# Order of weight and modulation-row requests on SyncE, four row buffers for the gate, and eviction order in group_a

## What is computed

```
shift, scale, gate = split(silu(c) @ w_mod + b_mod)      # w_mod: 2048 x 6144
h  = rms_norm(x) * (1 + scale) + shift
u, g = split(h @ w_in)                                   # 2048 each
pooled_i = window_mean(u_i) - u_i                        # 4 groups of 512 features
y  = (pooled_i @ w_grp_i) * pool_scale
x1 = x + gate * ((y * silu(g)) @ w_out)
x' = rms_norm(x1) * final_g
out = x' + hybrid_layer(x', mem)                         # attention a, b, c; not touched
```

## Time and profile before

| what | value |
|---|---|
| median of 3 runs | 2381.94 us (2381.07 to 2383.51) |
| the profiled execution, its own time | 2384.18 us |
| its span | 2382.6 us |
| mean granted TensorE clock | 0.982 |
| TensorE matmul busy | 2265.2 us, 95% of the span |
| VectorE busy | 1217.7 us, 51% |
| ScalarE busy | 844.8 us, 35% |
| DMA traffic | 280.39 MB, mean 118 GB/s |

### The profile page before, as it was taken

One profiled execution on the slowest core, in us unless ns is written; L12 is line 12 of the kernel. 1 busy time (PEld: TensorE's weight loads), 2 busy tenths in 40 slices (PEclk: granted clock), 3 DMA queues, 4 the chain that ended last, 5 costly groups with the idle time before them and its releaser, 6 DMA issues.

```text
span 2382.6 us, 31373 instructions
## 1 busy us (share of the span) xinstructions
PE 2265.2 (95%) x10156; PEld 1826.7 (77%) x10156; DVE 1217.7 (51%) x2102; ACT 844.8 (35%) x1551; POOL 149.6 (6%) x195
## 2 busy tenths in 40 slices
PE   5798779999899899999999999999999999999999
PEld 4686658887678677777777778888888888887887
DVE  6885567544665744444465656633433333334332
ACT  6433244433234333333344444422222222223221
POOL 0000000001122111111111111000000000000000
PEclk9999889999999999999999999999999999999999
DMA  8664412225643422222222222222222222222443
GB/s 327 242 232 159 174 65 98 98 98 201 236 154 108 148 82 79 76 74 79 71 71 69 73 67 88 84 98 97 97 96 97 96 94 95 96 96 87 148 147 110
DMA packets 74730, 280.39 MB, mean 118 GB/s; under 512 B 8596, under 2 KB 11412, under 8 KB 66208
## 3 DMA queue, kind: packets, MB, share of 16 engines
q1 hardware_dynamic: 68880, 263.59, 32.3%
q0 software_dynamic: 3040, 9.46, 1.1%
q10 hardware_dynamic: 2736, 6.42, 0.7%
HBM read 269.98 MB, written 9.46 MB: 117 GB/s over the span
## 4 chain that ended last, share of the span: by engine, by line
PE 81%; issue 7%; DVE 6%; DVEq 2%; ACT 2%; DMA 1%; ACTq 1%; SPq 0%; POOLq 0%; POOL 0%
PE bank L385 25%; PE bank L387 24%; PE bank L386 24%; DVE w_lo L379 3%; PE bank L467 3%; PE bank L497 2%; PE bank L481 1%; DVEq L374 1%; PE bank L505 1%; ACT w_hi L369 1%; DVE x_lo L1690 1%; DMA w_raw<-stream 0%; DVEq L1605 0%; DMA mem_raw<-mem_features 0%; PE bank L470 0%
## 5 line engine op out<-in xcount | busy, mean ns | idle before, releaser
L385 PE MATMUL bank<-x_hi,w_hi 128*128 128x512 f32 x2896 | 1166.8, 403 | 72.5 <-DVE w_lo L379 41.9
L387 PE MATMUL bank<-x_hi,w_lo 128*128 128x512 f32 x2896 | 1140.7, 394 | 0.0
L386 PE MATMUL bank<-x_lo,w_hi 128*128 128x512 f32 x2896 | 1140.6, 394 | 0.0
L379 DVE TENSOR_TENSOR w_lo<-w_raw,w_hi 128x512 fp32r<-128x512 f32 x692 | 490.2, 708 | 943.4 <-ACT w_hi L369 927.0
L369 ACT ACTIVATE w_hi<-w_raw 128x512 fp32r<-128x512 f32 x692 | 437.2, 632 | 1032.2 <-PE bank L387 920.4
L385 PEld LDWEIGHTS bank<-x_hi,w_hi 128*128 128x128 f32 x2896 | 552.0, 191 | 211.2 <-issue 42.8
L386 PEld LDWEIGHTS bank<-x_lo,w_hi 128*128 128x128 f32 x2896 | 552.4, 191 | 117.4 <-issue 6.3
L387 PEld LDWEIGHTS bank<-x_hi,w_lo 128*128 128x128 f32 x2896 | 551.3, 190 | 118.2
L1334 DVE CUSTOM_DVE_ANT_0 wmod<-wmod,c_rows 128x2048 f32<-128x2048 f32 x48 | 109.7, 2287 | 78.2 <-issue 78.2
L767 POOL TENSOR_TENSOR probs<-probs,rden 128x128 f32<-128x128 f32 (+2 forms) x112 | 79.7, 740 | 550.4 <-DVE rden L654 550.4
L565 ACT ACTIVATE probs<-probs,neg_max 128x128 f32<-128x128 f32 (+2 forms) x112 | 57.9, 517 | 95.5 <-DVE neg_max L642 95.2
(11 more groups left out here) (153 smaller groups left out, 1194.0 us busy)
## 6 DMA issues: line engine op xcount, KB each, us to landing
w_raw<-stream SPq DMA_DIRECT2D x346, 512.0 KB, 3.5
wmod<-w_mod_rows SPq DMA_DIRECT2D x48, 1024.0 KB, 6.6
front_raw<-stream SPq DMA_DIRECT2D x16, 1024.0 KB, 7.4
x<-x_features SPq DMA_DIRECT2D x4, 1024.0 KB, 18.4
x_in<-x_features SPq DMA_DIRECT2D x16, 256.0 KB, 4.7
x_store<-tmp POOLq DMA_DIRECT2D x16, 256.0 KB, 3.0
x_back<-x_store SPq DMA_DIRECT2D x16, 256.0 KB, 4.3
result_features<-result ACTq DMA_DIRECT2D x16, 256.0 KB, 4.1
```

Of the source, the lines that this page charges most:

```text
L379: nc.vector.tensor_tensor(w_lo[:, q, :], raw_quarter(s), w_hi[:, q, :].bitcast(F32), ALU.subtract).then_inc(lo_ready, 1)
L385: nc.tensor.matmul(bank_ap[:, :tokens], hi, x_hi[:, kx, :], start=start, stop=False)
L386: nc.tensor.matmul(bank_ap[:, :tokens], hi, x_lo[:, kx, :], start=False, stop=False)
L387: return nc.tensor.matmul(bank_ap[:, :tokens], lo, x_hi[:, kx, :], start=False, stop=stop)
```

## The change

In pool_u the two row requests of a panel are issued before the panel's load, not behind it. The gate's columns get four buffers (6 to 9) in place of two; at the start of pool_out four row requests are issued at once, and from m = 1 to 6 two each ahead of the panel's load. `c_rows` is kept: sq_b, sum_a and sum_b move into the region that the window sums no longer use, and `c_rows3` goes away with its load and its silu. Column 32 moves from beat (0, 3) to (0, 1). In group_a ScalarE runs `group_out` ahead of the two `h_high`. The variance in forget waits for both sums at once, since it now overwrites the place of sq_b.

```diff
-MOD_SLOT = [m % 4 for m in range(KT + 4)] + [2 + m % 4 for m in range(KT - 4)] + [6 + m % 2 for m in range(KT)]
+MOD_SLOT = [m % 4 for m in range(KT + 4)] + [2 + m % 4 for m in range(KT - 4)] + [6 + m % 4 for m in range(KT)]
...
-        sq_b = sb("sq_b", [P, T], F32, at_upper + 2 * KB)
-        sum_a = sb("sum_a", [P, T], F32, at_upper + 4 * KB)
-        sum_b = sb("sum_b", [P, T], F32, at_upper + 6 * KB)
+        sq_b = sb("sq_b", [P, T], F32, at_scratch + 4 * KB)
+        sum_a = sb("sum_a", [P, T], F32, at_scratch + 6 * KB)
+        sum_b = sb("sum_b", [P, T], F32, at_scratch + 8 * KB)
...
             for i in range(6):
-                load_panel(sp, At(RING + 1 + i))
                 mod_rows(KT + 4 + 2 * i)
                 mod_rows(KT + 5 + 2 * i)
+                load_panel(sp, At(RING + 1 + i))
...
             for m in range(KT):
+                if 0 < m < KT // 2 - 1:
+                    mod_rows(2 * KT + 2 * m + 2)
+                    mod_rows(2 * KT + 2 * m + 3)
                 load_panel(sp, At(FIRST["pool_out"] + 1 + m))
                 if m == 0:
                     sp.wait_ge(w_used, 4 * FIRST["pool_out"])
-                if m < KT // 2:
-                    mod_rows(2 * KT + 2 * m)
-                    mod_rows(2 * KT + 2 * m + 1)
+                    for n in range(4):
+                        mod_rows(2 * KT + n)
...
+                    if 4 * i + s > 0:
+                        group_out(4 * i + s - 1)
                     for k in range(4 + 2 * (4 * i + s), min(KT, 6 + 2 * (4 * i + s))):
                         h_high(k)
-                    if 4 * i + s > 0:
-                        group_out(4 * i + s - 1)
...
                     if m == 0 and s == 0:
                         gate_sigmoid(KT - 1)
-                        act.dma_start(c_rows3[:, :], cvec.to_broadcast([P, D])).then_inc(gate_c_loaded, 16)
                     if m == 0 and s == 1:
                         yg_high(KT - 1)
-                    if m == 0 and s == 2:
-                        act.wait_ge(gate_c_loaded, 16)
-                        nc.scalar.activation(c_rows3[:, :], c_rows3[:, :], ACT.Silu).then_inc(c_ready, 1)
                         act.preload_act_table_set("natural_log_exp_and_others")
...
-                    if m == 0 and s == 3:
-                        dve.wait_ge(c_ready, 2)
-                    if m < KT // 2 and s == (3 if m == 0 else 1):
-                        mod_column(2 * KT + 2 * m, c_rows3)
+                    if m < KT // 2 and s == 1:
+                        mod_column(2 * KT + 2 * m)
                     if m < KT // 2 and s == 3:
-                        mod_column(2 * KT + 2 * m + 1, c_rows3)
+                        mod_column(2 * KT + 2 * m + 1)
                         mod_biases(2 * KT + 2 * m, 2, 0.0)
...
                 if s == 3:
-                    dve.wait_ge(sums_full, 1)
+                    dve.wait_ge(sums_full, 2)
                     variance(score[0][:, :], T, D)
                     rstd_newton(dve, r_one[:, :], T, At(6))
-                    dve.wait_ge(sums_full, 2)
```

More of the change, by code:

```diff
@@ L241, in program @@
         at_mod = [at_x2, at_x2 + 8 * KB, at_x2 + 16 * KB, at_x2 + 24 * KB, at_x2 + 48 * KB, at_x2 + 56 * KB,
-                  at_x1 + 24 * KB, at_x1 + 56 * KB]
+                  at_x1 + 24 * KB, at_x1 + 56 * KB, at_x1 + 48 * KB, at_x1 + 16 * KB]
         wmod_sb = [sb(f"wmod{n}", [P, D], F32, at) for n, at in enumerate(at_mod)]
-        c_rows3 = sb("c_rows3", [P, D], F32, at_x1 + 16 * KB)
         front_raw = sb("front_raw", [P, 4, D], F32, at_x2 + 32 * KB)
@@ L291, in program @@
         hi_ready, lo_ready, w_used = sem("w_hi_ready"), sem("w_lo_ready"), sem("w_quarter_used")
-        wmod_loaded, wmod_used = [sem(f"wmod{n}_loaded") for n in range(8)], sem("wmod_used")
+        wmod_loaded, wmod_used = [sem(f"wmod{n}_loaded") for n in range(10)], sem("wmod_used")
         x_square_ready, x_square_added = sem("x_square_ready"), sem("x_square_added")
@@ L311, in program @@
         yg_made, yg_hi, yg_ready = sem("yg_made"), sem("yg_high_ready"), sem("yg_ready")
-        x_in_loaded, gate_c_loaded = [sem(f"x_in{n}_loaded") for n in range(2)], sem("gate_c_loaded")
+        x_in_loaded = [sem(f"x_in{n}_loaded") for n in range(2)]
         x1_ready, sq_ready, sq_added = sem("x1_ready"), sem("square_pair_ready"), sem("square_pair_added")
@@ L1327, in variance, with mod_column @@
                 nc.vector.tensor_scalar(var[:, :width], source, 1.0 / features, EPS, ALU.mult, ALU.add).then_inc(var_ready, 1)
-            def mod_column(m, c=c_rows):
+            def mod_column(m):
                 slot = MOD_SLOT[m]
                 dve.wait_ge(wmod_loaded[slot], 16 * (MOD_NTH[m] + 1))
-                nc.vector.memset(arrived[:, slot:slot + 1], 0.0)
-                nc.vector.tensor_tensor_reduce(out=wmod_sb[slot][:, :], in0=wmod_sb[slot][:, :], in1=c[:, :], scale=1.0,
+                nc.vector.memset(arrived[:, slot % 8:slot % 8 + 1], 0.0)
+                nc.vector.tensor_tensor_reduce(out=wmod_sb[slot][:, :], in0=wmod_sb[slot][:, :], in1=c_rows[:, :], scale=1.0,
                                                scalar=0.0, op0=ALU.mult, op1=ALU.add,
```

## The result

The changed kernel takes 2349.47 us, median of 4 runs (2347.85 to 2352.52), against 2381.61 us (4 runs, 2381.07 to 2383.51) for the kernel before on the same chip: ratio 0.987, 95% interval 0.9858 to 0.9881, so 32.1 us less. The forecast was 2337.5 with 2319 to 2354. The profiled execution took 2349.24 us, span 2347.7 at a mean granted clock of 0.987 (2382.6 at 0.982 before): by the traces alone 34.9 us less. TensorE is busy 2251.9 us, 96% of the span.

The account below looks back on a forecast made before the run. TensorE sets the pace at 2.72 us a quarter; some 85 us stand in three stages, with VectorE waiting for late rows. 32.2 + 5.5 + 7.0 - 0.3 = 44.4 us off 2381.9 gives 2337.5, range 2319 to 2354.

Parts of the forecast that it names:

- pool_u: Row requests one panel earlier let the stage run at TensorE's pace, with group_a's opening split at 285.0: 32.2 us less.
- B (DMA sets the pace): Rival for pool_u: late rows and half 0 make a panel 13.6 us, costing 16.3 us, total 2354; chance 0.11.
- C (requests serial): Rival: pool_u's requests each wait for the one before, 21.8 us a panel; slower than before, total 2422; chance 0.04.
- group_a: Eviction moved into ScalarE's wait for VectorE's addition: beats of 4.97 for 5.62 us, 5.5 us less up to gate_a.
- The opening stall: Start of pool_out: column 32 waits for rows until 8.1, delaying TensorE's fourth quarter by a new stall of 3.7 us.
- The loop of pool_out: Half 0 queues behind a row request awaiting a column: 14.5 us a panel, 36 quarters in 120.4, 7.0 us less.
- from column to column 4.45: Step in pool_out's loop: VectorE's time between a panel's two columns, 4.45 us of the 14.5 us turn.
- last slow start: Near the end of pool_out's 36 quarters: 1.3 us estimated, half of a quarter at the half clock.
- Rival A: Rows hidden in pool_out too: 103.4 us for the 36 quarters, 17 us less, total 2321; chance 0.10.
- No gain: Upper bound for pool_out: with a landing of 8.1 us the loop is 16.2 and the stage 127.
- forget: The variance waits for the second sum, ending at 766.54, where it started at 766.20: 0.3 us more.
- The case's own bounds: Range for the whole kernel's time from the forecast's bounds alone, without rivals: 2334 to 2347 us.

Follow-up runs that it names:

- alone on the chip: The kernel before with only SyncE's request order in pool_u changed, two rows ahead of the panel's halves: 2350.4 us against 2381.55, ratio 0.9865.
- column 32 later: The changed kernel with column 32 moved back behind the last split of panel 1, ahead of column 33: 2350.38 us, ratio 0.9872.
- rows behind the halves: The changed kernel with pool_out's two row requests from m = 1 on issued behind the panel's two halves, four buffers kept: 2322.49 us, ratio 0.9754.
- the squares a beat later: The changed kernel with ScalarE's squares of x1 for the first seven tiles moved from (m, 2) to (m + 1, 0): 2348.95 us, ratio 0.9865.
- all three edits: The changed kernel with pool_out's rows requested behind the halves, the first seven tiles' squares put off to panels 8 to 14, column 32 later: 2316.11 us.

## Why the prediction came out as it did

- **pool_u, right.** From its first split to group_a's opening split 120.1 us became 88.8 (196.35 to 285.12): 31.4 less, alone on the chip 31.2, forecast 32.2. The opening split stands at 285.12 for 285.0, which is closer than the term deserves: the stage began 0.75 us earlier in this trace (191.65 for 192.40), and the path was 0.8 longer than forecast. TensorE has 88.95 us for the stage, "87 to 90". Rivals B (DMA sets the pace) and C (requests serial) are out: TensorE is busy for all of the 88.95 us.
- **group_a, right.** Beats of 4.97; forecast 5.5 less, 6.0 in the trace and 5.9 on the chip.
- **The opening stall, right in place, 0.75 too long in size** (2.95 for 3.7): column 32 found its rows 7.5 us into the stage (522.46), where 8.1 was taken. That it was counted in full was of no weight: with the queue's loop behind it, it costs nothing (column 32 later).
- **The loop of pool_out, right in mechanism, wrong in one term.** The step that failed is "from column to column 4.45 (652.66 to 657.11)". It measured 6.39, and with it the turn 16.46 for 14.5; the landing was 6.5 for 6.4, and the first landing came at 38.7 for 37.9. Four periods of 1.96 more are 7.8 us and the first landing is 0.8. Some 0.6 is the last slow start: from 621.10 on TensorE has no gap, as forecast, but needs some 23.7 us for the two panels of 21.8 (granted clock 0.50 from 623 to 625), 1.9 more where 1.3 was taken. That makes 9.2 of the 9.5 us between 129.9 (127.4 and the 2.5 that the 64 quarters grew) and 120.4. I had taken 4.45 from a row in which VectorE first waited for rows, and so came to these instructions when GpSimd was done. The change removes just that wait. The duration was a measured one, but it held under a neighbour's timing that the change moves; a slow x_lo stood in the trace of before too, in panels without columns (GpSimd adds from 677.89 to 679.19 there), and I had not asked why:

```profile
677.93 1.81 DVE L1610 SCALAR_TENSOR_TENSOR x_lo<-x,hn_g,x_hi 128x512 fp32r<-128x512 f32 x1
```

- **Rival A, not met**, and the reason given was the right one: with the load ahead of the wait (rows behind the halves) the 64 quarters come to 178.8 (A's 103.4 for the first 36 and 28 of 2.72 make 179.6) and the total to 2322.5, where A said 2321.
- **"No gain" stood as the upper bound** (loop 16.2, stage 127), with the landing as its cause; the size was reached by another term. Nearly the whole miss is here: for pool_out and forget together 6.7 less was forecast and 4.7 more measured, 11.4 of the 12 us; pool_u gave 1.0 less than forecast and group_a 0.4 more.
- **forget, right**: by the traces, from forget's first split to the second sum it is 8.75 us before and 8.76 after, and from there up to the first matmul behind each of TensorE's next two waits it is 0.4 and 0.7 us more (765.52 to 782.21 and 794.91 before, 729.94 to 747.00 and 760.04 after), for 0.3. What the moved buffers do was not tried by itself.
- **The range, partly luck.** The case's own bounds gave 2334 to 2347, and 2349.5 lies outside them. The stated range reached to 2354 for rival B, DMA in pool_u, which was not met; its width covered the miss in pool_out by chance.
- **Three readings that bore nothing.** The rows at 242.94 were issued 0.4 us after VectorE's wait began (249.71 less 7.17 is 242.54), not before it. VectorE's waits for rows in pool_out were 4.4 to 7.2 us long from panel 1 on, not all "near 4.5". The 1.2 us that pool_u's sum takes off half 0 as its start is a guess that no row gives; pool_u went at TensorE's pace whatever it is.

## What the runs showed of the hardware

- **VectorE and GpSimd hold each other up where the VectorE instruction reads two tiles in SBUF.** Each w_lo and x_lo that starts while GpSimd adds ends about 0.55 us after that addition ends: w_lo 559.18 after 558.63, x_lo 560.88 after 560.33; in the kernel with the squares a beat later x_lo 576.48 after 575.93 and w_lo 578.19 after 577.63. From 510 to 760 us of the changed kernel 15 w_lo and 16 x_lo stand so as single rows of the timeline, all 0.54 to 0.56 us behind. The other way, an addition that starts within a column (556.53) ends 1.14 us after the column (557.49 to 558.63) and takes 2.10 us, where one that starts ahead of x_lo takes 1.35. The column itself takes 2.29 us with or without. The residual, which reads one tile in SBUF and one accumulator (bank), is not held: in the kernel with all three edits seven of them start within an addition and take the 0.74 or 0.75 us that they take elsewhere. VectorE, then GpSimd:

```profile
614.11 0.74 DVE L1602 SCALAR_TENSOR_TENSOR x<-bank,mod,x_in 128x512 f32<-128x512 f32 x1
...
613.59 1.75 POOL L1743 TENSOR_TENSOR sum_b<-sum_b,sq_b 128x512 f32<-128x512 f32 x1
```

  The Trainium skill (SBUF — State Buffer, Who interferes with whom) says that a VectorE instruction with two SBUF inputs contends with a GpSimd instruction that reads SBUF, that the port pair which the two share is an exclusive lock, and that issue order decides who blocks. By that rule, the traces agree, in both directions; w_lo, x_lo and the column each read two tiles in SBUF.
- **One core alone moved 405 GB/s from HBM over 18 us** (519 to 537 us of the changed kernel, DMA share 1.01), and 418 to 434 in the 2 us windows shown above. The Trainium skill (DMA: Bandwidth & Descriptors, Where 436 GB/s comes from) has some 358 GB/s, half of a stack's 716, as the limit for one core between HBM and SBUF. The measurement is higher, and decides for this case, in which only one core ran; no run here has two.

## What to carry to other kernels

More buffers let a request run ahead only if nothing that waits stands before it in its queue: in a queue that issues in order, put first the request whose buffer comes free first, and the one whose condition is long met behind it. Here the same part of the change, with its four buffers, cost 4.7 us with the rows ahead of the halves and gained about 22 with the rows behind (2344.66 to 2322.49). And a duration taken from a trace holds only with the neighbours it had: when a change takes a wait from an engine, look at what the others do at the new moment, above all GpSimd beside VectorE; then ask whether the lost time lies in a closed loop (1.94 us a turn cost 10 us) or in a lead that is never used up (it cost nothing).
